# Modulation loads between state-space chunks, decay arguments on ScalarE, the stage's tail reordered, a third place for a chunk's columns

## The reference, cut to what matters

```python
mod = (jax.nn.silu(c) @ w['w_ada'] + w['b_ada'])[:, None, :]
sh1, sc1, g1, sh2, sc2, g2 = jnp.split(mod, 6, axis=-1)
...
a_cs = jnp.cumsum(a, axis=-1)
Lm = jnp.exp(segsum(a))
cb = jnp.einsum('bcln,bcsn->bcls', Cc, Bc)
y_diag = jnp.einsum('bcls,bhcls,bcshp->bclhp', cb, Lm, xdt)
decay_states = jnp.exp(a_cs[..., -1:] - a_cs)
states = jnp.einsum('bcsn,bhcs,bcshp->bchpn', Bc, decay_states, xdt)
...
y_off = jnp.einsum('bcln,bchpn,bhcl->bclhp', Cc, new_states[:, :-1], jnp.exp(a_cs))
...
y = rmsnorm(y * jax.nn.silu(z.astype(F32)), norm_w)
```

## Time and profile before

| | us |
|---|---|
| median of 3 runs | 3592.61 (3580.4 to 3593.36) |
| profiled execution, its own time | 3585.37 |
| span of its trace | 3583.8 |
| busy: TensorE / VectorE / ScalarE / GpSimd | 3134.6 / 1587.7 / 1175.0 / 286.9 |
| chain that ended last: TensorE / VectorE / ScalarE / DMA | 76% / 8% / 5% / 3% |

### The profile page before, as it was taken

The page is one execution under the profiler, slowest core; times in us unless marked ns, Lnnn a source line. Parts: engine busy times, 40 slices in busy tenths (PEclk is TensorE's granted clock), DMA queues, the critical chain, the costliest instruction groups (busy, mean ns, idle before and its releaser), DMA issues.

```text
span 3583.8 us, 57577 instructions
## 1 busy us (share of the span) xinstructions
PE 3134.6 (87%) x20313; PEld 2681.3 (75%) x20313; DVE 1587.7 (44%) x3455; ACT 1175.0 (33%) x2069; POOL 286.9 (8%) x379
## 2 busy tenths in 40 slices
PE   3996677798989999999989777777888999999995
PEld 2993533364879999999989554335578999999994
DVE  3515669863342222322352465897534222222233
ACT  3212248764232212112132223785532321211211
POOL 1102032103000000000010103110120000000000
PEclk8997689897989999999999877999888999999997
DMA  5325045204211111111133413440151111111111
GB/s 186 81 41 221 14 125 169 84 2 162 80 36 41 48 46 46 47 47 43 42 81 66 167 54 108 147 136 1 60 165 36 47 44 45 46 47 47 47 42 48
DMA packets 276792, 268.20 MB, mean 75 GB/s; under 512 B 84392, under 2 KB 236446, under 8 KB 275312
## 3 DMA queue, kind: packets, MB, share of 16 engines
q1 hardware_dynamic: 242416, 154.65, 14.5%
q0 software_dynamic: 34192, 111.32, 10.0%
HBM read 248.21 MB, written 9.78 MB: 72 GB/s over the span
## 4 chain that ended last, share of the span: by engine, by line
PE 76%; DVE 8%; issue 6%; ACT 5%; DMA 3%; another core or an unknown queue 0%; DVEq 0%; POOL 0%; ACTq 0%; SPq 0%; POOLq 0%
PE bank L731 55%; PE bank L694 5%; PE bank L768 3%; ACT arena L1444 2%; PE bank L1125 2%; PE bank L1099 2%; DVE arena L1943 2%; DMA weights<-in_w_ada 2%; PE bank L1188 1%; PE bank L973 1%; DMA arena<-in_x_sample 1%; PE bank L1147 1%; PE bank L779 1%; PE bank L747 1%; PE bank L1065 1%
## 5 line engine op out<-in xcount | busy, mean ns | idle before, releaser
L731 PE MATMUL bank<-h_hi,w_hi 128*128 128x352 f32 x2736 | 883.4, 323 | 4.5 <-DVE w_lo L1567 4.5
L731 PE MATMUL bank<-h_lo,w_hi 128*128 128x352 f32 x2736 | 877.6, 321 | 0.0
L731 PE MATMUL bank<-h_hi,w_lo 128*128 128x352 f32 x2736 | 876.9, 321 | 0.0
L731 PEld LDWEIGHTS bank<-h_hi,w_hi 128*128 128x128 f32 x2736 | 513.8, 188 | 5.2 <-issue 5.1
L731 PEld LDWEIGHTS bank<-h_lo,w_hi 128*128 128x128 f32 x2736 | 514.6, 188 | 0.0
L731 PEld LDWEIGHTS bank<-h_hi,w_lo 128*128 128x128 f32 x2736 | 513.4, 188 | 0.0
L1567 DVE TENSOR_TENSOR w_lo<-weights,w_hi 128x1024 fp32r<-128x1024 f32 x186 | 227.8, 1225 | 611.7 <-ACT w_hi L1269 607.5
L731 PE MATMUL bank<-g_hi,w_hi 128*128 128x352 f32 x1392 | 450.5, 324 | 5.6 <-DVE arena L637 5.6
L731 PE MATMUL bank<-g_lo,w_hi 128*128 128x352 f32 x1392 | 447.4, 321 | 0.0
L731 PE MATMUL bank<-g_hi,w_lo 128*128 128x352 f32 x1392 | 447.0, 321 | 0.0
L694 PEld LDWEIGHTS bank<-arena 128*128 128x128 f32 (+4 forms) x1773 | 214.7, 155 | 240.0 <-issue 184.1
(11 more groups left out here) (330 smaller groups left out, 3694.4 us busy)
## 6 DMA issues: line engine op xcount, KB each, us to landing
weights<-in_w_ada SPq DMA_DIRECT2D x64, 512.0 KB, 7.0
weights<-in_w_gate SPq DMA_DIRECT2D x44, 512.0 KB
weights<-in_w_up SPq DMA_DIRECT2D x44, 512.0 KB, 3.8
weights<-in_w_in SPq DMA_DIRECT2D x66, 256.0 KB, 4.0
arena<-in_w_ada SPq DMA_DIRECT2D x32, 512.0 KB
weights<-in_w_down SPq DMA_DIRECT2D x32, 448.0 KB, 3.6
arena<-in_w_ada SPq DMA_DIRECT2D x8, 1024.0 KB, 17.5
weights<-in_w_down SPq DMA_DIRECT2D x16, 512.0 KB, 3.7
```

Source lines behind the costliest of these rows:

```text
L731: mm = pe.matmul(bank[:, 0:TC], wt[:, w], xt[:, x], start=(k + m == 0), stop=(k == n_k - 1 and m == 2))
```

## The change

- Of the 32 modulation units, 16 stay in stage 4. The other 16 go into stage 5, two behind the outputs of each prompt chunk, in bank 2 (`GB`); ring A has two banks meanwhile. Their rows and columns are read out at the end of stage 5.
- The differences' negative part is formed on ScalarE, as Relu of (sum minus row), ahead of the exponent, instead of by VectorE's L1782. `decay_in` is now given when the sums are there, and `decay_rows` is awaited by ScalarE. TensorE makes the rows ahead of the transposes.
- `STG` and `ACL` have three places; placing chunk c waits for the state of chunk c-3.
- The hardware loop is written out.
- The sample states are turned around chunk 6 and copied by ScalarE (`states_out`).
- In the tail VectorE's gate product for the prompt, the clearing of `O_QB` and the placing of queries come before the samples' outputs, and B's expansion has its own signal (`marked`).

```diff
             def modulate(at, k, h, into=YB):
...
-                for u in range(ADA_EARLY):
-                    if u == 2 * KD:
-                        pe.wait_ge(ada_rows, l * 3 + 2)
-                        modulation_turn(l * 3 + 2)
...
+                for u in range(2 * KD):
+                    modulation_part(u)
+                modulation_turn(l * 3 + 2)
...
-                with loop(pe, NB // 2 - 1, counts) as i:
-                    for t in range(2):
-                        decays(i * 2, t + 1, P, C("upper"), C("ones"))
-                        outputs(i * 2, t)
...
+                for c in range(NB - 1):
+                    decays(c + 1, P, C("upper"), C("ones"))
+                    if c == NB - 2:
+                        pe.wait_ge(s_state, l * 48 + 48)
+                        for q in range(2):
+                            states_turned(q)
+                    outputs(c)
+                    if c == NB - 2:
+                        for q in range(2, 4):
+                            states_turned(q)
+                    for u in range(2):
+                        modulation_part(2 * KD + 2 * c + u, GB)
...
+                act.wait_ge(state_ready, l * CHUNKS + max(c - 1, 1))
+                    act.wait_ge(decay_in, l * CHUNKS + (c + 1))
+                    act.wait_ge(decay_rows, l * CHUNKS + (c + 1))
+                    if c:
+                        act.wait_ge(chunk_mid, l * CHUNKS + c)
+                    for h in range(SH):
+                        step.only(act.activation(S(DM + n * h, n, 0, n), B(rows, [[1, n]], n * h, 0, n), ACT.Relu, bias=S(ACS + h, 1, 0, n), scale=-1.0))
+                    step.wait()
+                    act.activation(S(DM, 4 * n, 0, n), S(DM, 4 * n, 0, n), ACT.Exp, scale=-1.0)
...
-                    for h in range(SH):
-                        step.only(dve.tensor_scalar(S(DM + n * h, n, 0, n), B((XB, YB)[t % 2], [[1, n]], n * h, 0, n), S(ACS + h, 1, 0, n), 0.0, ALU.subtract, ALU.min))
...
-                for q in range(4):
-                    bank = Dr.next()
-                    read(dve.tensor_copy(S(STT_S + 512 * q, 512), bank[:, :]))
```

More of the change, by code:

```diff
@@ L890, in _, with decays @@
                 ended(pe, l, 4)
[L892 to L895 removed]
+                def decays(c, n, upper, last):
+                    pe.wait_ge(chunk_in, l * CHUNKS + (c + 1))
+                    stg, acl = STG[c % 3], ACL[c % 3]
                     bank = Dr.open()
@@ L1391, in exponentials, with states_out @@
                     act.activation(S(LDC, 4, 0, n), S(LDC, 4, 0, n), ACT.Exp).then_inc(decay_out, 1)
-                place_chunk(0, 0, P, u_tiles[:, :, 0:P], S(O_AT, 4))
-                place_chunk(0, 1, P, u_tiles[:, :, P:2 * P], S(O_AT + 4, 4))
-                exponentials(0, 0, P)
-                with loop(act, NB // 2 - 1, counts) as i:
-                    for t in range(1, 3):
-                        exponentials(i * 2, t, P)
-                        place_chunk(i * 2, t + 1, P, u_tiles[:, :, bass.ds(i * (2 * P) + (t + 1) * P, P)], dyn(O_AT + 4 * (t + 1), i, 8, 4))
-                exponentials(0, NB - 1, P)
-                place_chunk(0, NB, NS, u_tiles[:, :, SEQ:TOK], S(O_AT + 4 * NB, 4, 0, NS))
-                exponentials(0, NB, NS)
-                A.restart()
+                def states_out(first, last):
+                    for q in range(first, last):
+                        bank = A.next()
+                        A.done(act.activation(S(STT_S + 512 * q, 512), bank[:, :], ACT.Copy))
+                A.use(AB_FEW)
+                place_chunk(0)
+                place_chunk(1)
+                for c in range(CHUNKS):
+                    exponentials(c)
+                    if c + 2 < CHUNKS:
+                        place_chunk(c + 2)
+                    if c == NB - 2:
+                        states_out(0, 2)
+                    if c == NB - 1:
+                        states_out(2, 4)
+                modulation_rows(w_empty, l * ADA_USES + 4 * KD, GB, O_ADAT2)
+                modulation_columns(2)
+                A.use(AB)
                 ended(act, l, 5)
@@ L1778, in decays @@
                     bank = Dr.next()
-                    Dr.done(dve.tensor_copy(S(btk, P, 0, n), B(bank, [[1, P]], 0, 0, n)))
-                    dve.wait_ge(decay_rows, l * CHUNKS + c + (t + 1))
-                    for h in range(SH):
-                        step.only(dve.tensor_scalar(S(DM + n * h, n, 0, n), B((XB, YB)[t % 2], [[1, n]], n * h, 0, n), S(ACS + h, 1, 0, n), 0.0, ALU.subtract, ALU.min))
+                    read(dve.tensor_copy(S(btk, P, 0, n), B(bank, [[1, P]], 0, 0, n)))
                     if n == NS:
@@ L1818, in _ @@
                 dve.wait_ge(s_out, l * (N_OUT + 3) * 16 + N_OUT * 16)
[L1819 to L1827 removed]
+                decays(0, P, C("upper"), S(O_WT + 4, 4))
+                for c in range(NB):
+                    factors(c, P)
                     if c < NB - 1:
[L1829 removed]
+                        decays(c + 1, P, C("upper"), S(O_WT + 4 + 8 * (c + 1), 4))
                     else:
[L1831 removed]
+                        decays(NB, NS, C("upper_s", NS, 0, 0, NS), S(O_WT + 4 + 8 * NB, 4, 0, NS))
                     outputs(c, P, lambda j, c=c: S(H(4 + j, P * c), P))
```

151 lines of the change are left out of this document (71 added, 80 removed).

## The result

| | us |
|---|---|
| median after, 4 runs | 3534.84 (3524.85 to 3544.45) |
| median before, 4 runs beside them | 3592.99 (3580.4 to 3597.31) |
| ratio, with its 95% interval | 0.9844 (0.9804 to 0.9883) |
| the same pair once more, on another chip | 3527.12 against 3588.3, ratio 0.9826 (0.9813 to 0.984) |
| profiled execution after | 3544.45, span 3542.3 |

A forecast was written before the change was run, and what follows sets the result against it. Loads were taken to set stage 4's end, a latency chain around VectorE stage 5; terms summing to 43.3 off 3585.4 gave 3542.1, and half the difference to the median made it 3545. Ranges: 3525 to 3556 (chance 0.60), 3522 to 3569.

The forecast's parts named there:

- stage 4: VectorE's wait at the end of stage 4: sixteen modulation units leave TensorE's queue, gaining 7.2 and 5.9 us, together 13.1.
- first chunk: Start of stage 5: the table load stands exposed behind the Relus, a loss of 1.0 us per layer, -2.0.
- eight chunks: Stage 5: seven periods of 6.4 us and a first of 7.1, 51.8 against 56.9 and 61.0, gaining 14.3.
- tail, front part: From the eighth state's end to the samples' outputs: copies and expansion no longer ahead, gaining 4.0 us per layer, 8.0.
- tail, end: From the samples' outputs to the mark's end: 5.65 us falls to 0.7, gaining 9.9 for two layers.
- of which the six products at low clock are 4.69: End of stage 4: the pooling product keeps its 4.69 us, within 5.2 from its start to ScalarE's mark.
- the lower bound of 5.9: Chunk period in stage 5: forecast at 6.4 us, with bounds 5.9 and 6.6.
- buys next to nothing at high clock: Stage 5 chunks: moving L1782's 1.12 us off VectorE barely shortens the period, since TensorE's outputs stand beside it.
- A: Stage 5: the chunk chain gains nothing because a new hold-up takes what the loop gave; 3559 us, chance 0.14.
- B: Stage 5: TensorE's clock goes on changing, half the chunks at 9.6 us and half at 6.4; 3571, chance 0.11.
- C: Stage 5: TensorE stays at 1.2 GHz and becomes the bound, 9.6 us per chunk; 3599, chance 0.05.
- D: Period at 5.9 us (another 8 us) and part of the tail's products at high clock; 3533; below 3525 chance 0.07.

The follow-up runs named there:

- t_warm: Changed kernel plus three products of constants on TensorE ahead of stage 4's pooling product: VectorE's wait before stage 5 5.20 / 5.20 us, against 8.10 / 8.12.
- t_table: Changed kernel plus an early one-column exponent on ScalarE behind the first two placings: first chunk 5.08 / 4.51 us, against 6.40 / 6.39.
- u_dve: Changed kernel with the four differences back on VectorE instead of Relus on ScalarE: eight chunks 51.02 / 49.73 us, against 47.14 / 47.15.
- b_flat: Kernel before with only the hardware loop over chunks written out: eight chunks 53.51 / 53.90 us, against 56.97 / 60.97.
- u_mod4: Changed kernel with all 32 modulation units back in stage 4: eight chunks 50.07 / 49.88 us, against 47.14 / 47.15.
- u_two: Changed kernel with two places instead of three: eight chunks 48.50 / 48.27 us, against 47.14 / 47.15.
- b_relu: Kernel before with only the differences moved to ScalarE as Relus: eight chunks 62.27 / 60.22 us, against 56.97 / 60.97.
- u_tail: Changed kernel with gate product, clearing and query placing back behind the samples' outputs: tail 22.17 / 22.29 us, against 19.57 / 19.55.
- the additions: Changed kernel plus both the early one-column exponent and the three products of constants: median 3530.05 us, ratio to before 0.9836; changed kernel 3527.12 on that chip.
- t_warm5: The kernel of t_warm, unedited, timed over five rounds on another chip: 3474.93 us, ratio to the kernel before 0.9837.

## Why the prediction was right, and where it was off

The time (3545 against 3534.8, inside both ranges that the forecast gives) and the direction were right, and the gain was where it was said to be. That the sum came so near is in part luck: two terms were 6.0 us too favourable and three 11.1 us too small, and they offset each other. By its own steps, for two layers of the profiled executions:

| term | forecast | measured |
|---|---|---|
| stage 4 | 13.1 | 8.5 |
| first chunk | -2.0 | -3.4 |
| eight chunks | 14.3 | 23.6 |
| tail, front part | 8.0 | 9.3 |
| tail, end | 9.9 | 10.4 |
| sum | 43.3 | 48.5 |

*Stage 4.* The units did leave and the product started 0.13 us after VectorE's first mark. The step that failed is "of which the six products at low clock are 4.69". In the kernel before, the modulation and its transposes stood just ahead, and the clock rose during the product in the first layer, here cut in two at that point:

```profile
343.23:345.20 1.97, 1.97 (x5) 1.21 (x5) 0.00 (x0) 0.91 (x3) 0.00 (x0) 0.50 0.00 0
345.20:347.92 2.72, 2.72 (x9) 1.41 (x8) 0.00 (x0) 2.22 (x4) 0.00 (x0) 1.00 0.00 0
```

In the second layer all of its 3.72 us were at 2.4 GHz. Now it takes 6.82, and t_warm, with work ahead of it, 3.81. This takes 4.6 of the 13.1 us.

*First chunk.* The load is exposed and costs its own 1.28 us, which t_table gives back. On the rule that each load adds a drain of 1.38 us (the Trainium skill, "ScalarE: Activation LUTs", "What ACT_TABLE_LOAD costs") the trace disagrees for this place: the load starts 0.02 us after the last Relu, and the exponent 1.30 us after the load does. Of the 37 loads in the trace of the changed kernel 33 are followed by the next activation within 0.02 us. The further 0.7 are the rows at low clock: the Relus start 2.62 us after VectorE's first row, and 2.02 in t_warm; the forecast had 1.83.

*The chunks.* The mechanism was right (a regular chain, at high clock), the size was not: steady distances are 5.70, below the lower bound of 5.9, and not 6.4. The step that failed is the time from the outputs' start to the first read of them. It was taken as 1.75, nearer to a row in which VectorE's own differences stood in between; it is 1.18, by the lower bound's working. That is 0.57 of the 0.7; the rest are shorter gaps around the factors. With it falls the sentence that taking the differences off VectorE "buys next to nothing at high clock": u_dve puts it at 0.35 us a period.

The parts, each taken alone over both layers: the loop 10.5 (b_flat), the Relus 6.5 (u_dve), the modulation units between the chunks 5.7 (u_mod4), the third place 2.5 (u_two). They add up to 25.1 for 23.6. That does not show that they are independent: the loop was taken out of the kernel before and the others out of the changed one, each of the four has a change of the clock in it, and the Relus alone, from the kernel before, gave nothing (b_relu). The part of the units is all clock: the forecast saw them as a load on TensorE that must be hidden, and with them the clock in the chunks was 0.93 instead of 0.75.

*The tail.* Both terms held within 0.7 us a layer. The cover for the moved work was to be 2.1 us (8.9 less 6.8) and is 2.55 in the changed kernel; where TensorE was at high clock for the first groups of its products (t_warm) only 0.21 is left, so here the two engines are nearly even. u_tail gives 5.0 for the work that the forecast had at 5.6. The front part is read from the trace alone: no run puts the four copies of the sample states back on VectorE, and none puts the rows behind the transposes again.

*From the sum to the median.* The profiled execution after is 41 us under the one of before, not 48.5: the stages that the change leaves alone took 7 us more in it. One of these stages takes 158.5 us in the first layer and 153.6 in the second of the kernel before itself, so such a difference needs no effect of the change. The medians differ by 58 and 61 us, some 10 more than the two stages show in the traces. The forecast took the profiled execution of before as a fair one and added 3.6 us; the profiled execution of the changed kernel turned out to be the slowest of its set, both times.

*The rivals.* A (the chunks gain nothing) did not come: they take 47.1 us in either layer, where A leaves them at 57 and 61. B (the clock goes on changing) holds for two of the seven distances, 6.56 and 6.49, not for half of them, and the clock stood at 1.00 from the third chunk on and not from the second. The rule of the Trainium skill, "TensorE: Matmul & The Clock Gate", "Part 4: PE-mode transpose", that transposes do not count for the clock, is neither shown nor refuted: the chunks have other matmuls beside the transposes, and no kernel here parts the two. C (TensorE at 1.2 GHz as the bound, 9.6 a period) did not come. D comes nearest: 3533 for 3534.8, with more than forecast in the chunks, though its other part, tail products at high clock, is not in the trace of the changed kernel.

*What stays open.* Why the additions' 12.9 us are not in the median. The other executions of the changed kernel have a mean granted clock higher by 0.002 to 0.006, which with the low level at 0.50 means 14 to 42 us more at 2.4 GHz and, where TensorE is the bound, half of that in time, so 7 to 21 us. This would fit executions that lack the low clock at the pooling product or in the tail. Such layers exist in kernels that have this code unchanged: the wait ahead of stage 5 was 6.53 and 6.50 us in the second layers of u_two and t_table, where the others have about 8, and the tail 18.44 and 17.88 in their first layers, where the changed kernel has 19.57. But there is no trace of an execution other than the profiled one, so it is argued and not shown.

## What to carry to other kernels

In a chain of waits between engines, read the latency of a hand-over from a place where nothing else stands in between; a row in which the reader was busy itself gives only an upper bound, and here that was the largest miss. When work is taken out from ahead of a product, price that product at the clock of an engine that comes out of idle, and when work is put between the links of a chain, ask what it does to the clock and not only whether it fits. A gain that hangs on the clock in one profiled execution has to be timed over several: 12.9 us in the trace were nothing in the median.

## What the runs showed of the hardware that was not expected

- Less work for TensorE went with a slower chain: with the modulation units out of the chunks (u_mod4) TensorE was busy in 39.7 instead of 40.9 us, at clock 0.74 instead of 0.93, and the chunks took 2.9 us longer.
- Four Relus of 128 columns out of PSUM took 1.14 us together on ScalarE, the same as VectorE's four differences (1.12), so the move shifts the time and does not shrink it.
- The same kernel before took 3588 us on one chip and 3531 on another, with ratios of the kernels timed beside it at 0.983 to 0.984 on both. Between t_warm and t_warm5, one kernel on two chips, the difference lies in stages apart from those changed here.
